# Output columns of the second block added to x in two halves, steps at the layer seams and around the conv reordered, and two irregular weight groups laid out for one load a unit

## What is computed

```python
def hybrid_layer(x, ...):                      # twice (l = 0, 1)
    p = split_columns(rms_norm(x, pre_g) @ w_in + b_in)      # 6992 columns, 14 groups in the kernel
    o_sb, o_fox, o_mla = three kinds of attention on columns of p
    # nsa: keys and values are compressed first, by a 4096 -> 128 matrix each
    hidden = silu(blocks.reshape(B, n_cmp, 32 * 128) @ w1)   # w1_k and w1_v
    mix = concat([o_sb * silu(gate), o_nsa * ..., o_fox * ..., o_mla * ...])
    return x + rms_norm(mix @ w_out, post_g)

def second_block(x, ...):
    proj = rms_norm(x, norm1_g) @ w_in_2
    out_a = dilated_mixture(aq, ak, av)        # 8 heads of 64
    out_b = conformer_conv(bu, bg, ...)        # u * sigmoid(gate), 31 taps over time, layer norm, silu
    out_c = band_attention(cq, ck, cv, sinks)  # 16 heads of 64
    x = x + concat([out_a, out_b, out_c]) @ w_out_2
    h2 = rms_norm(x, norm2_g)
    return x + (silu(h2 @ w_gate) * (h2 @ w_up)) @ w_down
```

## Time and profile before

| | |
|---|---|
| Runs | 2085.05, 2084.08, 2081.74 us |
| Profiled execution: its time | 2084.3 us |
| its span, first to last instruction | 2082.7 us |
| TensorE matmul busy | 2012.2 us (97%), 10370 matmuls |
| VectorE busy | 1123.3 us (54%) |
| ScalarE busy | 931.3 us (45%) |
| GpSimd busy | 76.8 us (4%) |
| Mean granted TensorE clock | 0.989 of full |
| DMA | 360.80 MB, mean 173 GB/s |

### The profile page before, as it was taken

How to read it: one execution, slowest core, us unless ns; L and a number is a source line. 1 busy time by engine, 2 the same in 40 slices (tenths; PEclk the granted TensorE clock), 3 DMA queues, 4 the chain that set the end, 5 groups by cost and what they waited for, 6 DMA issues and landing times.

```text
span 2082.7 us, 27966 instructions
## 1 busy us (share of the span) xinstructions
PE 2012.2 (97%) x10370; PEld 1712.6 (82%) x10370; DVE 1123.3 (54%) x1309; ACT 931.3 (45%) x1215; POOL 76.8 (4%) x126
## 2 busy tenths in 40 slices
PE   7999999998999999998999887999999999999998
PEld 6889988887789998887888766888888888888886
DVE  4474555555556464554647864644445544444443
ACT  5355434444454444444554434444444444433442
POOL 3000000001100000001100100000000000000000
PEclk9999999999999999999999999999999999999999
DMA  7584455665665444665545423566666666656553
GB/s 256 163 251 124 137 167 157 186 198 147 201 195 188 140 155 127 206 187 152 169 152 152 129 74 122 181 192 186 189 191 191 191 183 190 191 187 207 202 202 112
DMA packets 209513, 360.80 MB, mean 173 GB/s; under 512 B 22641, under 2 KB 45728, under 8 KB 209152
## 3 DMA queue, kind: packets, MB, share of 16 engines
q1 hardware_dynamic: 203728, 345.36, 54.3%
q0 software_dynamic: 4816, 13.76, 2.3%
q10 hardware_dynamic: 864, 0.27, 0.1%
HBM read 357.23 MB, written 2.10 MB: 173 GB/s over the span
## 4 chain that ended last, share of the span: by engine, by line
PE 90%; DVE 3%; ACT 2%; DMA 1%; issue 1%; SPq 1%; DVEq 1%; ACTq 0%; POOL 0%; POOLq 0%
PE psum L551 24%; PE psum L553 24%; PE psum L552 24%; PE psum L559 3%; PE psum L561 3%; PE psum L562 3%; DVE wl L522 1%; DMA raw<-in_w_in_dram 1%; SPq L506 1%; PE psum L627 1%; DVE conv_y L766 1%; PE psum L867 1%; PE psum L641 1%; PE psum L616 1%; ACT wh L515 1%
## 5 line engine op out<-in xcount | busy, mean ns | idle before, releaser
L522 DVE TENSOR_TENSOR wl<-raw,wh 128x1024 fp32r<-128x1024 f32 (+2 forms) x672 | 797.4, 1197 | 735.9 <-ACT wh L515 728.9
L515 ACT ACTIVATE wh<-raw 128x1024 fp32r<-128x1024 f32 (+2 forms) x672 | 690.5, 1036 | 879.4 <-PE psum L553 712.1
L551 PE MATMUL psum<-wh,xh 128*128 128x512 f32 (+2 forms) x1600 | 623.7, 390 | 1.2 <-DVE xl L809 1.2
L553 PE MATMUL psum<-wh,xl 128*128 128x512 f32 (+2 forms) x1600 | 616.7, 385 | 0.0
L552 PE MATMUL psum<-wl,xh 128*128 128x512 f32 (+2 forms) x1600 | 616.5, 385 | 0.0
L551 PEld LDWEIGHTS psum<-wh,xh 128*128 128x128 f32 x1600 | 302.3, 189 | 62.6 <-DVE xl L809 2.9
L553 PEld LDWEIGHTS psum<-wh,xl 128*128 128x128 f32 x1600 | 301.9, 189 | 59.5
L552 PEld LDWEIGHTS psum<-wl,xh 128*128 128x128 f32 x1600 | 302.6, 189 | 57.4
L551 PE MATMUL psum<-wh,mh 128*128 128x512 f32 x384 | 153.3, 399 | 18.0 <-issue 9.8
L553 PE MATMUL psum<-wh,ml 128*128 128x512 f32 x384 | 152.2, 396 | 0.0
L552 PE MATMUL psum<-wl,mh 128*128 128x512 f32 x384 | 152.0, 396 | 0.0
(11 more groups left out here) (342 smaller groups left out, 1509.7 us busy)
## 6 DMA issues: line engine op xcount, KB each, us to landing
raw<-in_w_in_dram SPq DMA_DIRECT2D x264, 512.0 KB, 4.3
raw<-in_w_out_dram SPq DMA_DIRECT2D x96, 512.0 KB, 3.7
raw<-in_w_gate_dram SPq DMA_DIRECT2D x88, 512.0 KB, 3.6
raw<-in_w_up_dram SPq DMA_DIRECT2D x88, 512.0 KB, 3.6
raw<-in_w_down_dram SPq DMA_DIRECT2D x80, 512.0 KB, 4.1
bias<-in_b_in_dram POOLq DMA_DIRECT2D x18, 256.0 KB, 4.0
raw<-in_w_in_dram SPq DMA_DIRECT2D x16, 268.0 KB, 2.8
raw<-in_nsa_cmp_w_k_dram SPq DMA_DIRECT2D x32, 128.0 KB, 2.3
```

The lines of the kernel that those rows point to most:

```text
L515: act.activation(wh[:, n % SPLIT_SLOTS, 0:k, 0:unit.n], raw[:, n % RAW_SLOTS, 0:k, 0:unit.n], ACT.Copy).then_inc(hi_done, 1)
L522: dve.tensor_tensor(out=wl[:, n % SPLIT_SLOTS, 0:k, 0:unit.n], in0=raw[:, n % RAW_SLOTS, 0:k, 0:unit.n], in1=wh[:, n % SPLIT_SLOTS, 0:k, 0 ...
L551: pe.matmul(o, ah_[:, kt, tok], hi_w, start=first, stop=False)
L553: ins = pe.matmul(o, al_[:, kt, tok], hi_w, start=False, stop=last)
```

## The change

It leaves the computation as it is. Its parts:

- **Loads.** The host lays the 336 small columns of `w_in` out as one matrix `w_small`, and the four quarters of the compression weights side by side as `cmp_w1`. A unit of either is then one load.
- **Start.** SyncE loads x block 0, units 0 and 1, then x block 1, unit 2, and so on. Eight constants move from ScalarE's queue to SyncE's, behind the load of unit 7; GpSimd's seven constants wait until the last block of x is there.
- **Layer seams.** The splits of the next layer's first three units come before the last mid. The last output unit is multiplied by token block (`by_rows`), so that ScalarE can square the first block early. The sums of three groups are made ahead, GpSimd does one operation in place of two. The first block of x is updated in two halves, and only that block is turned before the first unit.
- **Second block, stages 1 to 15.** The scaling of the first queries, its transposes and three other mids move by a slot; two taps leave slot 12; ScalarE copies all of `probT2` in three mids.
- **Second block, output.** All four groups start with pairs 4 to 7 (16 units in slots 16 to 23), are added to x, and the pairs 0 to 3 of each are added to x again in slots 23 to 28. The conv's rows are waited for by the semaphore `conv_rows2` at one unit, no longer by a mid. Taps move to units of slots 16 and 17 and behind mid 18.

```diff
+SMALL_COLUMNS = ((3072, 268), (5388, 4), (6416, 64))
+N_SMALL = sum(w for _, w in SMALL_COLUMNS)
...
-    units = [Unit("cmp_w1", tuple((c, HD) for c in range(0, 4 * HD, HD)), (2 * j, 2 * j + 1), "cmp", None, "cmp",
+    units = [Unit("cmp_w1", ((0, 4 * HD),), (2 * j, 2 * j + 1), "cmp", None, "cmp",
...
-    slots = [[unit(0, 4)], [unit(0, 5)], [unit(1, 4), unit(1, 5)], [unit(0, 6)], [unit(0, 7), unit(1, 6)], [unit(1, 7)],
-             [], [unit(0, 0), unit(0, 1), unit(1, 0), unit(1, 1)], [unit(0, 2), unit(0, 3)],
-             [unit(1, 2), unit(1, 3), rest[0], rest[1]]]
-    slots[7][0].after_mid = 22
-    slots[8][0].after_mid = 23
-    slots[9][2].after_mid = 24
-    return slots + slots_of(rest[2:])
+    def early(g, *pairs):
+        return [output_unit("w_out_2", g, pair, 7, 4) for pair in pairs]
+
+    def late(g, *pairs):
+        return [output_unit("w_out_2", g, pair, 3, 0) for pair in pairs]
+    slots = [early(0, 4, 5), early(1, 4, 5), early(0, 6, 7) + early(1, 6), early(1, 7), early(2, 4, 5, 6),
+             early(2, 7), early(3, 4), early(3, 5, 6, 7) + late(0, 0, 1), late(0, 2, 3) + late(1, 0, 1),
+             late(1, 2, 3), late(2, 0, 1, 2, 3), late(3, 0, 1), late(3, 2, 3)]
+    slots[7][3].after_mid = 22
+    slots[8][0].after = "conv_rows2"
+    slots[8][2].after_mid = 23
...
+            if unit.after is not None:
+                pe.wait_ge(s(unit.after), 1)
...
+            if unit.by_rows:
+
+                for tb in range(TB):
+                    tok = slice(tb * P, (tb + 1) * P)
+                    for kk, kt in enumerate(unit.kts):
+                        o, hi_w, lo_w = out_[:, tb, 0:unit.n], wh[:, slot, kk, 0:unit.n], wl[:, slot, kk, 0:unit.n]
+                        pe.matmul(o, ah_[:, kt, tok], hi_w, start=False, stop=False)
+                        pe.matmul(o, ah_[:, kt, tok], lo_w, start=False, stop=False)
+                        ins = pe.matmul(o, al_[:, kt, tok], hi_w, start=False, stop=kk == len(unit.kts) - 1)
+                    ins.then_inc(s("first_rows") if tb == 0 else unit_used, 1)
+                return
...
-                for b in {0: (0, 1), 2: (2,), 5: (3,)}.get(n, ()):
+                for b in {0: (0,), 1: (1,), 3: (2,), 5: (3,)}.get(n, ()):
...
-                        if l == 0 and n < BLOCKS:
-                            load_x(n)
+                        if l == 0 and n in (0, 2, 3, 4):
+                            load_x(max(n - 1, 0))
                         load_unit(sp, place, n, unit, layer_src(l))
+                        if l == 0 and n == PARTS - 1:
+                            for dst, name in CONSTS[POOL_CONSTS:]:
+                                sp.dma_start(dst, d[name]).then_inc(consts_loaded, 16)
...
-                pool_rstd(place.once, "post", [(slice(0, TB), DM)])
+
+                pool.wait_ge(s("post_sums"), place.once)
+                stand_alone(pool, "pool")
+                pool.tensor_tensor(out=rstd[:, 0:TB], in0=sq_sums[:, 0:TB], in1=minus_half.to_broadcast([P, TB]),
+                                   op=ALU.pow).then_inc(s("post_rstd"), 1)
...
-                1: turn_conv_weights, 2: lambda: turn_pairs(cqn, 0), 4: turn_c_keys, 5: lambda: c_scores(0, 0),
+                1: turn_conv_weights, 3: lambda: turn_pairs(cqn, 0), 4: turn_c_keys, 5: lambda: c_scores(0, 0),
...
-                26: lambda: turn_final_x(range(0, 8)), 28: lambda: turn_final_x(range(8, EARLY_KT)),
+                26: lambda: turn_final_x(range(0, 8)), 27: lambda: turn_final_x(range(8, EARLY_KT)),
...
+                def ahead_of_last():
+                    next_splits(l)
+                    act.wait_ge(s("first_rows"), place.once)
+                    output_squares(3, [0])
...
-            taps_at_unit = {first_tap_unit + SLOT_UNITS * i + n: 1 for i, m in enumerate((4, 4, 3, 3, 3)) for n in range(m)}
-            taps_at_mid = {9: 2, 15: 3, 16: 4, 17: 2, 18: 3}
+            taps_at_unit = {first_tap_unit + SLOT_UNITS * i + n: 1 for i, m in enumerate((4, 2, 3, 3, 3)) for n in range(m)}
+            taps_at_unit.update({first_tap_unit + 5 * SLOT_UNITS + n: 1 for n in range(4)})
+            taps_at_mid = {9: 2, 15: 1, 16: 4, 18: 5}
...
+            after_unit[CONV_UNIT] = conv_low
             slots_with_mids(place, SLOTS_2, {
-                1: first_queries, 3: kv_group,
+                1: first_queries, 2: lambda: head_scale("cq02", 0, 512, split_heads(cqn)), 3: kv_group,
...
-                11: lambda: (head_sums("aq2", 512), sinks_max("c10", 8), head_scale("aq2", 1, 512, split_heads(aqn)), sinks_sum("c10")),
-                12: lambda: (dve_copy_half(probT2)),
+                11: lambda: (sinks_max("c10", 8), head_sums("aq2", 512), sinks_sum("c10")),
+                12: lambda: head_scale("aq2", 1, 512, split_heads(aqn)),
...
-                17: lambda: (softmax_max("a0"), softmax_sum("a0")), 18: lambda: dve_copy_half(probT2),
-                19: lambda: (softmax_max("a4"), small_out(o_a, 0), softmax_sum("a4")),
+                17: lambda: (softmax_max("a0"), softmax_sum("a0")),
+                18: lambda: add_output(0),
+                19: lambda: (softmax_max("a4"), small_out(o_a, 0), softmax_sum("a4"), add_output(1)),
...
-                22: lambda: (conv_sumsq(), dve_mix_low(place, "a", mh2, ml2, 0, 0)), 23: conv_low,
-                24: lambda: add_output(0), 25: lambda: add_output(1), 26: lambda: final_x_low(range(0, 8), 1),
-                27: lambda: add_output(2), 28: lambda: final_x_low(range(8, EARLY_KT), 2), 29: last_output,
+                22: lambda: (conv_sumsq(), add_output(2), dve_mix_low(place, "a", mh2, ml2, 0, 0)),
+                23: lambda: add_output(3),
+                24: lambda: add_output(0), 25: lambda: add_output(1),
+                26: lambda: (add_output(2), final_x_low(range(0, 8), 1)),
+                27: lambda: final_x_low(range(8, EARLY_KT), 2), 28: last_output,
...
+    given["w_small"] = np.concatenate([given["w_in"][:, :, c0:c0 + w] for c0, w in SMALL_COLUMNS], axis=2)
+
+    halves = [given[name].reshape(LAYERS, 2, CMP_STRIDE * P, HD) for name in ("nsa_cmp_w1_k", "nsa_cmp_w1_v")]
+    given["cmp_w1"] = np.concatenate([h[:, half] for half in range(2) for h in halves], axis=2)
```

More of the change, by code:

```diff
@@ L111, in input_units, with unit @@
 def input_units(weight, groups):
-    return [Unit(weight, pieces, (2 * j, 2 * j + 1), layout, g % 2, "x", KT, j == 0, j == KT // 2 - 1)
-            for g, (_, pieces, layout) in enumerate(groups) for j in range(KT // 2)]
+    def unit(name, pieces, g, layout, j):
+        source, pieces = ("w_small", ((0, N_SMALL),)) if name == "nsa_win_small" else (weight, pieces)
+        return Unit(source, pieces, (2 * j, 2 * j + 1), layout, g % 2, "x", KT, j == 0, j == KT // 2 - 1)
+    return [unit(name, pieces, g, layout, j) for g, (name, pieces, layout) in enumerate(groups)
+            for j in range(KT // 2)]
 def output_unit(weight, g, pair, last_pair, first_pair=0):
@@ L134, in output_slots @@
     units[6].after_mid = NG * 2
+    units[-1].by_rows = True
     return slots_of(units)
 def output_slots_2():
-    def unit(g, pair):
-        return output_unit("w_out_2", g, pair, 3, 4)
-    rest = [output_unit("w_out_2", g, pair, 7) for g in (2, 3) for pair in range(8)]
-    slots = [[unit(0, 4)], [unit(0, 5)], [unit(1, 4), unit(1, 5)], [unit(0, 6)], [unit(0, 7), unit(1, 6)], [unit(1, 7)],
-             [], [unit(0, 0), unit(0, 1), unit(1, 0), unit(1, 1)], [unit(0, 2), unit(0, 3)],
-             [unit(1, 2), unit(1, 3), rest[0], rest[1]]]
-    slots[7][0].after_mid = 22
-    slots[8][0].after_mid = 23
-    slots[9][2].after_mid = 24
-    return slots + slots_of(rest[2:])
+    def early(g, *pairs):
[8 more added lines that the diff above has]
+    slots[8][2].after_mid = 23
+    return slots
 CMP_SLOTS = (6, 7)
@@ L162 @@
 UNITS_2 = sum(len(s) for s in SLOTS_2)
+CONV_UNIT = sum(len(s) for s in SLOTS_2[:WIN_SLOTS_2 + 8]) + 1
 FFN_STEPS = DFF // GN
@@ L836, in act_first @@
                     act_norm(name, scratch, updates, n - 6)
-                split_high(place, n, units[n])
+                ahead = n + 1 if updates else n
+                if ahead < PARTS:
+                    split_high(place, ahead, units[ahead])
                 act_operand(place, name, n)
@@ L841, in dve_first, with operand, split @@
             nc.vector.wait_ge(norm_g_loaded, 16 * (updates + 1))
-            split_low(place, 0, units[0])
+            def operand(n):
+                dve_operand(place, name, n)
+            def split(n):
+                split_low(place, n, units[n])
+            if not updates:
+                for n in range(2):
+                    operand(n)
+                    split(n)
+                for n in range(2, PARTS):
+                    split(n)
+                    operand(n)
+                return
             update(0)
+            operand(0)
+            operand(1)
             update(1)
-            dve_operand(place, name, 0)
-            for n in range(1, PARTS):
```

(29 more changed lines are left out.)

105 lines of the change are left out of this document (60 added, 45 removed).

## The result

The changed kernel takes 2056.16 us (median of four runs, 2052.3 to 2057.68), the kernel before 2084.57 in the same comparison. The ratio is 0.9863, with a 95% interval of 0.9846 to 0.988: 28.4 us faster. I predicted 2050, so the time lies 6 us above the forecast and inside the range of 2042 to 2062.

The account below looks back on a forecast made before the run. TensorE, busy 97% of the span, was taken as the bound, so only its waits and half-clock time could be won. Gains of 1.4 + 7.0 + 3.0 + 4.0 + 18.7 = 34.1 from 2084.3 gave 2050 us, range 2042 to 2062.

Parts of the forecast that it names:

- The likeliest case: Whole kernel: the forecast of 2050 us with its own range of 2043 to 2058, chance 0.53.
- Output, -18.7: Second block from slot 12: of 35.2 us of waits and lost clock 16.5 remain, a gain of 18.7 us.
- Slots 15 to 18: 4.7: Second block, slots 15 to 18: VectorE needs 26.1 us against TensorE's 20.7, so 4.7 us of waiting stays.
- Two falls of the clock: Second block from slot 12: two half-clock windows behind the waits above 3 us, 1.7 us each, 3.4 together.
- Stage 2, -4.0: Second block, first queries' transposes: the 2.3 us wait and the 1.7 lost at half clock go.
- One load a unit, -7.0: Compression and small units: fewer issues on SyncE cut 8.9 us of waits to 2, between -9 and -4.
- the ring of four raw buffers: Limit left after merging loads: 6.2 us per buffer against 5.6 for four units, about 1 us a layer.
- rival 2: Slot 7: merged loads give nothing because raw buffers or transfers limit, 7.0 us less gain, 2057 us, chance 0.12.
- waits for the low part: Sign of a wrong prediction: slot 7 keeps a transfer share near 1 and TensorE waits for VectorE's low operand.
- Seams, -3.0: Two layer seams: TensorE stands 4.9 us for 5.75 and loses less clock, 3.0 us gained, between -6 and +1.
- half of the 2.6 at the lower clock gone: First layer seam: half of the 2.6 us lost at the lower clock disappears, part of that seam's -2.2.
- Start, -1.4: Kernel start: unit 0 begins about 1.6 us earlier, some lost again, 1.4 us gained, between -3 and 0.

Follow-up runs that it names:

- seam_undone: The changed kernel with both layer seams in the order of the kernel before, the start still changed: 2053.89 us, ratio 0.9848 to the kernel before.
- before_merged: The kernel before with only the merged small and compression loads (`w_small`, `cmp_w1`) added: 2082.19 us, ratio 0.9988 to the kernel before.

## Why the prediction was right, and where not

The likeliest case was the right one in its sum (2056 in its own range of 2043 to 2058) and in the gains of the second block. That the sum came within 6 us is in part luck: the loads alone missed by 9.4 us, the seams by 1.1 and the start by 0.4 the same way, while 2.3 us that I hadn't foreseen and 1.0 at the output made up for some of it.

- **Output, -18.7; the trace has -19.7.** Stage 12: 1.0 predicted, 1.08 found. Slots 15 to 18: 4.7 predicted, 2.9 found at slot 18; my walk took every step at full length with no lead, which may be why. Mids 18 and 19: 1.1 and 1.1 against 0.99 and 0.56 + 0.50. The conv: 3.6 against 3.17. Last turns: 1.4 against 1.08. Two falls of the clock were predicted and found, but they cost 4.6 us and not 3.4, since the one behind the conv lasts 6.8 us. Undoing the parts one at a time costs 4.3, 4.7 and 10.0 us.
- **Stage 2, -4.0:** the wait and the lower clock are gone.
- **One load a unit, -7.0: this step failed.** "What remains is the ring of four raw buffers: load (about 4 us)": beside the broadcasts the load takes 7.5, and the step has no word of GpSimd's queue. Slots 6 and 7 came out 2.4 us worse in the trace, outside the term's own bounds of -9 to -4. The merged loads alone gained 2.1 us; with the broadcasts gone they gain 7.8, and the waits fall to 2.1, near the 2 that I had left for the ring. So the size of the term was right once nothing else limited slot 7, and rival 2 ("the transfers are the limit in slot 7") came true for another reason than its own. Its share of 0.88 was read in a window that ends as the broadcasts start. The Trainium skill, "DMA: Bandwidth & Descriptors", Specifications, by whose reading the merge gains about nothing, gave an estimate of the total (2057) nearer to the result, but not for its reason: without the broadcasts the merge gains 7.8, although the pieces of 128 columns are rows of 512 B. How much of that is issues and how much data rate is open. The prediction had named "waits for the low part" in slot 7 as a sign of being wrong, and that sign came.
- **Seams, -3.0:** 3.1 + 1.4 + 0.4 us of waiting predicted, 3.00 + 1.05 + 0.31 found. What failed is "half of the 2.6 at the lower clock gone": it stayed 2.5, and at the second seam 1.4 became 2.4, as the stretch there is now 6.8 us long and was 3.4 before. The chip's time doesn't show even the 1.9 us of the trace.
- **Start, -1.4:** unit 0 began at 10.62, near the 10.45 that I had worked out, but behind a wait of 2.44 us, where the kernel before waits 2.34 for the second block of x; only the 0.66 ahead of unit 1 went, and the sum of waits fell by 0.5. Unit 0 is early because the turn of the second block now stands behind it and not ahead of it. That gave another 0.5, as at 15.5 us the same eight transposes take half the time (before, then after):

```profile
10.44 1.97 PE L790 MATMUL psum<-ident,x 128*128 128x128 f32 x8 [2.34 <-DMA x<-in_x_dram]
...
15.54 1.04 PE L813 MATMUL psum<-ident,x 128*128 128x128 f32 x8
```

  A wait of 0.20 us that both kernels have later ends at 34.91 after and at 35.87 before, so the start gave 1.0.
- **Not foreseen, -2.3:** stage 2 of a layer waited 1.3 us in each (the turn of the latents). In `seam_undone` the wait is back in the second layer (1.5) but not in the first (0.2), which has no seam ahead of it; and in `before_merged`, with the old seams, it is 0.4 and 0.3. So the seam's order is not the whole cause, and how much it did is open.

## What to carry to other kernels

Before pricing a stretch by its own queue, list every DMA in flight there, small ones of other engines too. When a limit is taken away, ask in the trace how far behind the next one stands; the median of an edit that moves a wait looks like that of one that does nothing. A small load that stands in the busiest stretch of a kernel is worth its own buffer and an early place.
